# Four split weight blocks in a ring at all times, in place of two, with the new slots in the scratch of dynamic DMAs

## The chip, the cores and the metric

The kernel runs on one core of a Trainium2 chip. The metric is the device time of one execution in microseconds (us). TensorE (PE in the profile) multiplies matrices, VectorE (DVE) and ScalarE (ACT) do elementwise work, GpSimd (POOL) here does nothing but split weights, and SyncE (SP) issues the loads of weights. Each engine runs its own program; they meet at semaphores.

## What is computed

One inference step of a two-layer hybrid decoder trunk over 544 tokens (512 of a prompt, 8 x 4 of samples), in fp32. The reference, cut to its frame:

```python
def _swiglu(x, w_gate, w_up, w_down):
    return (jax.nn.silu(x @ w_gate) * (x @ w_up)) @ w_down

def _layer(x, state, p):
    f = _swiglu(_rmsnorm(x, p['ffn1_norm_pre']), p['ffn1_w_gate'], p['ffn1_w_up'], p['ffn1_w_down'])
    x = x + (0.5 * _rmsnorm(f, p['ffn1_norm_post'])).astype(x.dtype)
    m, new_state = _token_mixer(_rmsnorm(x, p['mix_norm_pre']), *state, p)
    x = x + _rmsnorm(m, p['mix_norm_post']).astype(x.dtype)
    f = _swiglu(_rmsnorm(x, p['ffn2_norm_pre']), p['ffn2_w_gate'], p['ffn2_w_up'], p['ffn2_w_down'])
    x = x + (0.5 * _rmsnorm(f, p['ffn2_norm_post'])).astype(x.dtype)
    return x, new_state
```

`_token_mixer` projects to the inputs of three recurrent branches (gated DeltaNet, GLA, Mamba-2), runs them, projects each branch's output, merges them by sigmoid gates and projects once more. The model width is 1024, the width of the feed-forward part 2816.

## The kernel before, in words

**Blocks.** Activations lie transposed in SBUF: 128 partitions of channels, 544 tokens along the free axis. A weight matrix is cut into blocks of up to 128 x 1024: eight tiles k of 128 x 128 that share one tile of output channels. To keep fp32 accuracy each operand is held as a rounded high part and a low part that is left over, and each tile takes six matmuls of 272 columns (`products`, lines 625 to 629): high by high, high by low, low by high, each for two halves of the tokens. A full block is 48 matmuls, a narrow one (tiles of the small columns, 128 x 256) is 12, a merge block (128 x 768) 36.

**The way of a block.** SP loads it into one of four slots of `raw` (512 KB for a full one). POOL splits it in two instructions: a conversion `wh<-raw` (TENSOR_SCALAR, line 586 or 572) and a subtraction `wl<-raw,wh` (TENSOR_TENSOR, line 588 or 574), which counts up `lo_done`. TensorE waits for `lo_done`, multiplies, and its last matmul counts up `blk_done`, which frees the split slot. `wh` and `wl` have two slots, so POOL may split block b+2 when block b is done.

**Two more slots for a while.** At the start of a feed-forward part TensorE takes three blocks side by side, tile k by tile k, because tile k of the input is ready before tile k+1. For that `whx` and `wlx` give slots to blocks 2 and 3. They lie in the memory of `al`, the low part of the feed-forward's inner activations, so they are free only behind the last block of the projection down of the part before. `first_blocks` on POOL splits these four blocks, in the order of FIRST_ORDER: 0, 1, 2, 3 in FFN 1 and 2, 3, 0, 1 in FFN 2, where `al` has been free since the merge.

**The order of the stages** in a layer, by its blocks: FFN 1 with 44 blocks up (gate and up in turn) and 24 down (a third of a tile row each: 8, 8, 6 tiles); the projection with 4 narrow blocks and 40 wide ones; the recurrent branches, in which no block is used and whose scratch covers `raw`, `wh` and `wl`; 48 merge blocks; 8 of the out projection (`wout`); FFN 2 like FFN 1.

**Borders between stages.** There TensorE waits for VectorE and ScalarE. VectorE scales and adds the result (`f` line 1951, `x` line 1956), and makes the low part `hl` of the next input (line 1931 in front of a feed-forward part, lines 1906 and 1912 in front of the projection, line 2525 in front of the merge). `xsq` (line 1942) sums the squares for the norm; TensorE takes its last tile through a matmul (line 693) in the middle of block 3 of the part up. In front of the merge the last updates of `states` (line 2205) must be four on before TensorE starts.

**Semaphores.** `blk_done` starts at SPLIT, and every wait that counts finished blocks adds SPLIT, so the same expressions hold for any depth of the ring.

Of the kernel before, what the change touches and what calls it, by code (L numbers as in the profile page):

```python
# [7 lines left out]
P = 128  # L8
# [5 lines left out]
KD = D_MODEL // P  # L14
# [46 lines left out]
RAW, SPLIT = 4, 2  # L61
# [82 lines left out]
FIRST_ORDER = (0, 1, 2, 3), (2, 3, 0, 1)  # L144


def split_count(which, j):

    return FIRST_ORDER[which].index(j) + 1

# [32 lines left out]
def trunk(nc, io):  # L183
    ctx = ExitStack()
    with ctx:
# [17 lines left out]

        x = put("x", [P, KD, T])
        RING = place[0]
        raw = put("raw", [P, RAW, KD, P])
        wh = put("wh", [P, SPLIT, KD, P], F32R)
        wl = put("wl", [P, SPLIT, KD, P], F32R)
# [230 lines left out]
        def _(sp_):  # L439
# [121 lines left out]
        def _(pool):  # L561
            def first_blocks(layer, which, first):

                for j in FIRST_ORDER[which]:
                    src = raw[:, j, :, :].rearrange("p k m -> p (k m)")
                    hi, lo = (a.rearrange("p k m -> p (k m)") for a in split_of(j, True))
                    pool.wait_ge(raw_full[j], layer * (BLOCKS // RAW * 16) + 16 * (first // RAW + 1))
# [4 lines left out]
                    pool.tensor_scalar(hi, src, 1.0, 1.0, MULT, MULT).then_inc(hi_done, 1)  # L572
                    pool.wait_ge(hi_done, layer * BLOCKS + first + split_count(which, j))
                    pool.tensor_tensor(lo, src, hi.bitcast(F32), SUB).then_inc(lo_done, 1)

            def blocks(layer, first, i, nks):

                for j, nk in enumerate(nks):
                    src = raw[:, j % RAW, 0:nk, :].rearrange("p k m -> p (k m)")
                    hi, lo = (a[:, 0:nk, :].rearrange("p k m -> p (k m)") for a in split_of(j, False))  # L580
# [29 lines left out]
        def _(pe):  # L610
            pe.wait_ge(first_in, 32)

            def products(j, slot, ks, moving, start, stop, ready=None, ahead=False, between=None):

                for n, k in enumerate(ks):
# [7 lines left out]
                    high, low = (w[:, k, :] for w in split_of(j, ahead))  # L623
# [8 lines left out]
            def product(layer, first, i, j, per, slot, nk, moving, start=True, stop=True, ready=None, ahead=False, between=None):  # L632
# [3 lines left out]
                products(j, slot, range(nk), moving, start, stop, ready, ahead, between).then_inc(blk_done, 1)  # L636
# [44 lines left out]
            def ffn(layer, which, first):  # L681

                def up(i, js=range(4)):
                    for j in js:

                        pe.wait_ge(prod_done if j % 2 else sil_done, value(pe, layer * (2 * KF) + i * 2 + (which * KF + j // 2 + 1)))
                        product(layer, first, i, j, 4, j, KD, h_tiles, ahead=i is FIRST,
                                between=all_squares if i is FIRST and j == 3 else None)
# [2040 lines left out]
```

## Time and profile before

| | before |
|---|---|
| median of 3 runs | 3318.38 us (3314.03 to 3329.16) |
| span of the profiled execution, first to last instruction | 3324.6 us |
| TensorE busy | 3162.4 us, 95% |
| VectorE busy | 1309.5 us, 39% |
| ScalarE busy | 776.6 us, 23% |
| GpSimd busy | 1577.5 us, 47% |
| HBM read | 243.70 MB |

The profiler took one execution. Its time is given as the span alone, which lies between the lowest and the highest of the timed runs. A busy share is a mean over stages; what a stall costs is read at its place. Matmuls overlap in the profile, so the mean duration of one (about 290 ns) is longer than the distance from one to the next (about 126 ns).

### The profile page before, as it was taken

The numbers are of one execution on the slowest core, as the hardware profiler recorded it, in microseconds if no ns is written. First come the engines' busy times: TensorE is split into PE (matmuls) and PEld (weight loads), VectorE is DVE, ScalarE is ACT, GpSimd is POOL, SyncE is SP. The second block draws the span as 40 slices with busy tenths as digits, with TensorE's granted clock in tenths as the row PEclk, the third lists the DMA queues.
The fourth block names the chain that finished last, engine by engine and source line by source line (L and its number), as shares of the span: only waits on it lengthen the run. The fifth ranks groups of instructions, "written<-read, shape, count | busy, mean of one in ns | idle before, by whom it ended". The sixth has DMA issues, their size and how long they took to land.

```text
span 3324.6 us, 67286 instructions
## 1 busy us (share of the span) xinstructions
PE 3162.4 (95%) x26882; PEld 3059.8 (92%) x26882; DVE 1309.5 (39%) x1984; ACT 776.6 (23%) x1523; POOL 1577.5 (47%) x948
## 2 busy tenths in 40 slices
PE   7999989999989998999999999999999899999997
PEld 7999979987769998999989999899877799899997
DVE  4331064637752225331053311735487422343311
ACT  2111033324441112111021111343344311221100
POOL 4665545620016664555546655556100256555553
PEclk9999999999979999999999999999999799999999
DMA  3222222200132222222222222222002322222221
GB/s 136 83 88 84 75 78 85 83 25 2 41 136 89 86 91 76 88 88 83 83 81 88 88 87 72 79 83 89 7 2 73 121 89 90 96 70 88 86 83 67
DMA packets 78589, 261.08 MB, mean 79 GB/s; under 512 B 8640, under 2 KB 10816, under 8 KB 77632
## 3 DMA queue, kind: packets, MB, share of 16 engines
q1 hardware_dynamic: 78112, 257.82, 24.0%
q8 instruction: 149, 2.44, 0.3%
q10 hardware_dynamic: 288, 0.49, 0.1%
q14 instruction: 40, 0.33, 0.0%
HBM read 243.70 MB, written 14.58 MB: 78 GB/s over the span
## 4 chain that ended last, share of the span: by engine, by line
PE 86%; DVE 8%; ACT 4%; issue 2%; DMA 0%; POOL 0%; DVEq 0%; SPq 0%; ACTq 0%; POOLq 0%
PE ps L625 25%; PE ps L627 25%; PE ps L629 25%; PE ps L766 1%; PE ps L727 1%; DVE cacc L2012 1%; PE ps L649 1%; DVE l_att L2265 1%; DVE x L1956 1%; PE ps L1032 1%; PE ps L976 1%; DVE f L1951 1%; ACT states L1495 0%; PE ps L759 0%; PE ps L1275 0%
## 5 line engine op out<-in xcount | busy, mean ns | idle before, releaser
L586 POOL TENSOR_SCALAR wh<-raw 128x1024 fp32r<-128x1024 f32 (+2 forms) x456 | 465.4, 1021 | 1636.4 <-PE ps L629 1107.4
L588 POOL TENSOR_TENSOR wl<-raw,wh 128x1024 fp32r<-128x1024 f32 (+2 forms) x456 | 1051.7, 2306 | 67.2 <-POOL wh L586 0.3
L625 PE MATMUL ps<-hh,wh 128*128 128x272 f32 x4768 | 998.2, 291 | 76.5 <-DVE hl L1931 25.8
L627 PE MATMUL ps<-hl,wh 128*128 128x272 f32 x4768 | 992.2, 290 | 0.0
L629 PE MATMUL ps<-hh,wl 128*128 128x272 f32 x4768 | 990.7, 289 | 0.0
L625 PEld LDWEIGHTS ps<-hh,wh 128*128 128x128 f32 x4768 | 755.8, 190 | 84.8 <-issue 55.8
L629 PEld LDWEIGHTS ps<-hh,wl 128*128 128x128 f32 x4768 | 755.3, 190 | 0.0
L627 PEld LDWEIGHTS ps<-hl,wh 128*128 128x128 f32 x4768 | 753.0, 189 | 0.0
L629 PE MATMUL ps<-ah,wl 128*128 128x272 f32 x1408 | 291.3, 288 | 0.0
L625 PE MATMUL ps<-ah,wh 128*128 128x272 f32 x1408 | 291.3, 288 | 0.0
L627 PE MATMUL ps<-al,wh 128*128 128x272 f32 x1408 | 291.1, 288 | 0.0
L1985 DVE TENSOR_TENSOR prod<-sil,ps 128x544 f32<-128x544 f32 x88 | 63.5, 721 | 421.2 <-PE ps L629 401.6
L1942 DVE TENSOR_TENSOR sq<-sq 128x544 f32<-128x544 f32 x36 | 31.3, 871 | 499.9 <-ACT sq L1436 499.9
L629 PEld LDWEIGHTS ps<-ah,wl 128*128 128x128 f32 x1408 | 221.6, 189 | 0.0
L625 PEld LDWEIGHTS ps<-ah,wh 128*128 128x128 f32 x1408 | 221.6, 188 | 0.0
L627 PEld LDWEIGHTS ps<-al,wh 128*128 128x128 f32 x1408 | 220.3, 188 | 0.0
L1991 DVE TENSOR_TENSOR al<-prod,ah 128x544 f32 x88 | 145.1, 1648 | 97.0 <-ACT ah L1451 97.0
L2012 DVE SCALAR_TENSOR_TENSOR cacc<-pad,cw,cacc 128x568 f32<-128x568 f32 x120 | 169.4, 1412 | 12.6
L1451 ACT ACTIVATE ah<-prod 128x544 f32 x88 | 58.1, 660 | 464.6 <-DVE prod L1987 464.6
L1436 ACT ACTIVATE sq<-ps 128x544 f32 x48 | 30.0, 625 | 553.3 <-PE ps L629 553.3
L2564 DVE TENSOR_TENSOR sg<-ps,rstd 128x544 f32<-128x544 f32 x48 | 34.8, 724 | 252.1 <-PE ps L629 252.1
L1982 DVE TENSOR_TENSOR sil<-ps,rstd 128x544 f32<-128x544 f32 x88 | 63.7, 724 | 146.8 <-PE ps L629 120.7
(430 smaller groups left out, 3552.0 us busy)
## 6 DMA issues: line engine op xcount, KB each, us to landing
raw<-in_up SPq DMA_DIRECT2D x176, 512.0 KB, 3.5
raw<-in_win SPq DMA_DIRECT2D x80, 512.0 KB, 3.5
raw<-in_merge SPq DMA_DIRECT2D x96, 384.0 KB, 3.0
raw<-in_down SPq DMA_DIRECT2D x64, 512.0 KB, 3.5
raw<-in_down SPq DMA_DIRECT2D x32, 384.0 KB, 3.1
raw<-in_wout SPq DMA_DIRECT2D x16, 512.0 KB, 3.4
states<-in_in_gdn SPq DMA_DIRECT2D x2, 2048.0 KB, 8.9
proj<-in_in_ssd SPq DMA_DIRECT2D x2, 2048.0 KB, 9.9
```

The lines of the kernel that those rows point to most:

```text
L586: pool.tensor_scalar(hi, src, 1.0, 1.0, MULT, MULT).then_inc(hi_done, 1)
L588: pool.tensor_tensor(lo, src, hi.bitcast(F32), SUB).then_inc(lo_done, 1)
L625: pe.matmul(out, high, mh_[:, c], start=a, stop=False)
L627: pe.matmul(out, high, ml_[:, c], start=False, stop=False)
L629: last = pe.matmul(out, low, mh_[:, c], start=False, stop=b)
L649: last = pe.matmul(ps[:, 6 + h, 0:HALF], ones, src[:, h * HALF:(h + 1) * HALF], start=start, stop=stop, skip_group_check=True)
L1451: act.activation(ah[:, bass.ds(i * 2 + j, 1), :].rearrange("p k t -> p (k t)"), prod[:, j, :], ACT.Copy).then_inc(ah_done, 1)
L1982: dve.tensor_tensor(halves(sil[:, j, :]), pair(2 * j), halves(rstd[:, :]), MULT).then_inc(gate_done, 1)
L1985: dve.tensor_tensor(halves(prod[:, j, :]), halves(sil[:, j, :]), pair(2 * j + 1), MULT).then_inc(prod_tmp, 1)
L1991: dve.tensor_tensor(al[:, m, :].rearrange("p k t -> p (k t)"), prod[:, j, :], ah[:, m, :].rearrange("p k t -> p (k t)").bitcast(F32), SUB) ...
L2012: last = dve.scalar_tensor_tensor(out=a, in0=pad[:, j, t:t + CW], scalar=cw[:, 4 * j + t:4 * j + t + 1], in1=a, op0=MULT, op1=ADD)
L2564: dve.tensor_tensor(halves(sg[:, u % 2, :]), pair(2 * u % 4), halves(rstd[:, :]), MULT).then_inc(gate_done, 1)
```

## The change

The ring has four split slots throughout. `whx` and `wlx` get memory of their own, 16 KB per partition, ahead of `x`. They hold slots 2 and 3; `wh` and `wl` keep 0 and 1. The room comes from the scratch that the program reserves for dynamic DMAs, set to 512 in the program's constructor. With four slots everywhere, block j of any stage goes to slot j % 4, POOL may split block b+4 when block b is done, and the special case at the start of a feed-forward part goes: `first_blocks` on POOL, FIRST_ORDER and `split_count`, and the four single loads on SP at the start of FFN 2.

```diff
-RAW, SPLIT = 4, 2
+RAW, SPLIT = 4, 4
...
-FIRST_ORDER = (0, 1, 2, 3), (2, 3, 0, 1)
...
+        whx, wlx = (put(s, [P, 2, KD, P], F32R) for s in ("whx", "wlx"))
         x = put("x", [P, KD, T])
...
-        whx, wlx = (at(s, R + 44 * TB + 8192 * i, [P, 2, KD, P], F32R) for i, s in enumerate(("whx", "wlx")))
-        assert 2 * 8192 <= 8 * TB
-
-        def split_of(j, ahead):
-            return (whx[:, j - 2], wlx[:, j - 2]) if ahead and j >= 2 else (wh[:, j % SPLIT], wl[:, j % SPLIT])
+        def split_of(j):
+            j %= SPLIT
+            return (whx[:, j - 2], wlx[:, j - 2]) if j >= 2 else (wh[:, j], wl[:, j])
...
-                if which:
-                    for j in range(4):
-                        sp_.wait_ge(lo_done, layer * BLOCKS + first + split_count(which, j) + RAW)
-                        ups(layer, which, first, 1, slice(j, j + 1))
-                with sp_.Fori(2 if which else 1, KF // 2) as i:
+                with sp_.Fori(1, KF // 2) as i:
                     ups(layer, which, first, i)
...
-                    if which and j >= SPLIT:
-                        pool.wait_ge(blk_done, layer * BLOCKS + B_OUT + SPLIT)
-                    else:
-                        pool.wait_ge(blk_done, layer * BLOCKS + first + min(j + 1, SPLIT))
...
             def ffn(layer, which, first):
-                first_blocks(layer, which, first)
+                blocks(layer, first, 0, (KD,) * 4)
...
-    nc = bacc.Bacc("TRN2", target_bir_lowering=False, num_devices=1)
+    nc = bacc.Bacc("TRN2", target_bir_lowering=False, num_devices=1, dynamic_dma_scratch_size=512)
```

No instruction is added or taken away on POOL or TensorE; the wait on `blk_done` in front of each conversion asks for two blocks less. At the start of FFN 2 the order of the splits changes too. On POOL, behind the loop over the out projection, before the change (`whx` and `wlx` are slots 2 and 3, in the memory of `al`):

```order
L572 TENSOR_SCALAR whx_70<-raw_50 128x1024 [waits blk_done,raw_full2]
L574 TENSOR_TENSOR wlx_71<-raw_50,whx_70 128x1024 [waits hi_done]
L572 TENSOR_SCALAR whx_70<-raw_50 128x1024 [waits blk_done,raw_full3]
L574 TENSOR_TENSOR wlx_71<-raw_50,whx_70 128x1024 [waits hi_done]
L572 TENSOR_SCALAR wh_51<-raw_50 128x1024 [waits blk_done,raw_full0]
L574 TENSOR_TENSOR wl_52<-raw_50,wh_51 128x1024 [waits hi_done]
L572 TENSOR_SCALAR wh_51<-raw_50 128x1024 [waits blk_done,raw_full1]
L574 TENSOR_TENSOR wl_52<-raw_50,wh_51 128x1024 [waits hi_done]
```

And at the same place after it:

```order
L561 TENSOR_SCALAR wh_53<-raw_52 128x1024 [waits blk_done,raw_full0]
L563 TENSOR_TENSOR wl_54<-raw_52,wh_53 128x1024 [waits hi_done]
L561 TENSOR_SCALAR wh_53<-raw_52 128x1024 [waits blk_done,raw_full1]
L563 TENSOR_TENSOR wl_54<-raw_52,wh_53 128x1024 [waits hi_done]
L561 TENSOR_SCALAR whx_49<-raw_52 128x1024 [waits blk_done,raw_full2]
L563 TENSOR_TENSOR wlx_50<-raw_52,whx_49 128x1024 [waits hi_done]
L561 TENSOR_SCALAR whx_49<-raw_52 128x1024 [waits blk_done,raw_full3]
L563 TENSOR_TENSOR wlx_50<-raw_52,whx_49 128x1024 [waits hi_done]
```

The four blocks are now split in their order, and each waits for one block of the out projection. At the end of the narrow blocks, in front of the wide ones, POOL's rows before the change are:

```order
L586 TENSOR_SCALAR wh_51<-raw_50 128x256 [waits blk_done,raw_full2]
L588 TENSOR_TENSOR wl_52<-raw_50,wh_51 128x256 [waits hi_done]
L586 TENSOR_SCALAR wh_51<-raw_50 128x256 [waits blk_done,raw_full3]
L588 TENSOR_TENSOR wl_52<-raw_50,wh_51 128x256 [waits hi_done]
L600 UNCONDITIONAL_BRANCH
```

And after it:

```order
L561 TENSOR_SCALAR whx_49<-raw_52 128x256 [waits blk_done,raw_full2]
L563 TENSOR_TENSOR wlx_50<-raw_52,whx_49 128x256 [waits hi_done]
L561 TENSOR_SCALAR whx_49<-raw_52 128x256 [waits blk_done,raw_full3]
L563 TENSOR_TENSOR wlx_50<-raw_52,whx_49 128x256 [waits hi_done]
L575 UNCONDITIONAL_BRANCH
```

The order is the same; narrow blocks 2 and 3 have slots of their own, and the first wide block shares its slot with narrow block 0 in place of narrow block 2. At the merge it is likewise: blocks 2 and 3 go to `whx` and `wlx`, which no branch uses as scratch, and wait for no merge block.

## Rows read from the trace of the kernel before

**Rows 1.** The page, parts 1 and 3: engines' busy time, and the main DMA queue

```profile
PE 3162.4 (95%) x26882; PEld 3059.8 (92%) x26882; DVE 1309.5 (39%) x1984; ACT 776.6 (23%) x1523; POOL 1577.5 (47%) x948
...
q1 hardware_dynamic: 78112, 257.82, 24.0%
```

**Rows 2.** Windows: us; busy us (count) of PE, PEld, DVE, ACT, POOL; PEclk; DMA

```profile
1300.00:1650.00 350.00, 350.00 (x2778) 350.00 (x2777) 80.19 (x83) 45.88 (x63) 207.74 (x120) 1.00 0.28 87
```

**Rows 3.** POOL's instructions grouped by shape: count, busy us, mean ns, idle

```profile
L588 POOL TENSOR_TENSOR wl<-raw,wh 128x1024 fp32r<-128x1024 f32 x320 | 808.4, 2526 | 47.5 <-POOL wh L586 0.2
L586 POOL TENSOR_SCALAR wh<-raw 128x1024 fp32r<-128x1024 f32 x320 | 349.0, 1091 | 806.4 <-PE ps L629 806.4
L588 POOL TENSOR_TENSOR wl<-raw,wh 128x768 fp32r<-128x768 f32 x128 | 236.1, 1845 | 19.0 <-POOL wh L586 0.2
L586 POOL TENSOR_SCALAR wh<-raw 128x768 fp32r<-128x768 f32 x128 | 111.3, 869 | 772.7 <-DMA raw<-in_merge 528.9 <-PE ps L629 243.8
```

**Rows 4.** TensorE's waits: us in total, times, longest

```profile
PE ps L625 <- DVE states L2205: 17.0, 2, 8.6
...
PE ps L625 <- DVE hl L1912: 12.5, 9, 3.9
...
PE ps L625 <- POOL wl L588: 2.8, 2, 1.6
```

**Rows 5.** Windows: narrow blocks of layer 1, and the start of the merge

```profile
2097.60:2101.30 3.70, 3.67 (x16) 3.65 (x17) 3.03 (x6) 0.66 (x1) 1.66 (x2) 0.54 0.60 203
...
976.60:981.20 4.60, 4.59 (x20) 4.59 (x21) 2.35 (x4) 0.00 (x0) 0.00 (x0) 0.50 0.41 171
```

**Rows 6.** Lines 1982 and 1987: duration in ns, min/median/max

```profile
L1982 DVE TENSOR_TENSOR sil<-ps,rstd x88: 709/724/727, 42.9 to 3164.3; 128x544 f32<-128x544 f32 x88
...
L1987 DVE TENSOR_TENSOR prod<-prod,rstd x88: 724/725/2417, 46.6 to 3171.2; 128x544 f32<-128x544 f32 x88
```

**Rows 7.** The chain that ended last: start us, us, ahead of FFN 2 and FFN 1

```profile
1248.29 1.12 DVE f L1951
...
1249.44 2.76 DVE x L1956
...
1662.38 1.44 DVE x L1956
1663.82 2.81 DVE f L1951
1666.63 1.47 DVE hl L1931
```

**Rows 8.** Timeline of DVE and PE: narrow blocks, first wide block, layer 0

```profile
445.13 0.72 DVE L1912 TENSOR_TENSOR hl<-hf,hh 128x544 fp32r<-128x544 f32 x1
...
450.48 2.23 DVE L1912 TENSOR_TENSOR hl<-hf,hh 128x544 fp32r<-128x544 f32 x2
...
452.76 0.52 PE L625 MATMUL ps<-hh,wh 128*128 128x272 f32 x2 [0.43 <-DVE hl L1912]
...
455.07 0.49 PE L625 MATMUL ps<-hh,wh 128*128 128x272 f32 x2 [1.28 <-POOL wl L588]
```

**Rows 9.** Timeline of DVE and PE: start of FFN 2, layer 0

```profile
1269.38 5.27 DVE L1942 TENSOR_TENSOR xsq<-xsq 128x544 f32<-128x544 f32 x7
...
1276.20 1.14 PE L693 MATMUL ps<-xsq,cst 128*128 128x240 f32 x6
```

**Rows 10.** Timeline of POOL and PE: in front of the merge, layer 0

```profile
969.02 1.88 POOL L588 TENSOR_TENSOR wl<-raw,wh 128x768 fp32r<-128x768 f32 x1
...
976.61 0.82 PE L625 MATMUL ps<-hh,wh 128*128 128x272 f32 x2 [8.44 <-DVE states L2205]
```

**Rows 11.** Tile raw, 955 to 975 us: issues of loads, time to landing

```profile
L450 SPq DMA_DIRECT2D raw<-in_merge x4: 344/431/527, 961.1 to 962.5; - x4
...
DMA to landing us min/median/max: 3.0/5.5/7.2
```

**Rows 12.** Tile nt_s, 965 to 975 us: durations in ns, min/median/max

```profile
L2456 DVE SCALAR_TENSOR_TENSOR nt_s<-nt_s,prm,nrs_s x4: 238/520/1787, 968.1 to 969.2; 128x32 f32<-128x32 f32 x4
```

More of the change, by code:

```diff
@@ L206, in trunk @@
         raw = put("raw", [P, RAW, KD, P])
-        wh = put("wh", [P, SPLIT, KD, P], F32R)
-        wl = put("wl", [P, SPLIT, KD, P], F32R)
+        wh = put("wh", [P, 2, KD, P], F32R)
+        wl = put("wl", [P, 2, KD, P], F32R)
         cst = put("cst", [P, NCONST])
@@ L561, in _ @@
         def _(pool):
[L562 to L567, printed above, removed]
-                    if which and j >= SPLIT:
-                        pool.wait_ge(blk_done, layer * BLOCKS + B_OUT + SPLIT)
-                    else:
-                        pool.wait_ge(blk_done, layer * BLOCKS + first + min(j + 1, SPLIT))
-                    pool.tensor_scalar(hi, src, 1.0, 1.0, MULT, MULT).then_inc(hi_done, 1)
-                    pool.wait_ge(hi_done, layer * BLOCKS + first + split_count(which, j))
-                    pool.tensor_tensor(lo, src, hi.bitcast(F32), SUB).then_inc(lo_done, 1)
             def blocks(layer, first, i, nks):
@@ L579, in blocks @@
                     src = raw[:, j % RAW, 0:nk, :].rearrange("p k m -> p (k m)")
-                    hi, lo = (a[:, 0:nk, :].rearrange("p k m -> p (k m)") for a in split_of(j, False))
+                    hi, lo = (a[:, 0:nk, :].rearrange("p k m -> p (k m)") for a in split_of(j))
                     turns = len(nks) // RAW
@@ L611, in _, with products @@
             pe.wait_ge(first_in, 32)
-            def products(j, slot, ks, moving, start, stop, ready=None, ahead=False, between=None):
+            def products(j, slot, ks, moving, start, stop, ready=None, between=None):
                 for n, k in enumerate(ks):
@@ L622, in products @@
                     halves_of = [(ps[:, 2 * slot + h, 0:HALF], slice(h * HALF, (h + 1) * HALF)) for h in range(2)]
-                    high, low = (w[:, k, :] for w in split_of(j, ahead))
+                    high, low = (w[:, k, :] for w in split_of(j))
                     for out, c in halves_of:
@@ L630, in products, with product @@
                 return last
-            def product(layer, first, i, j, per, slot, nk, moving, start=True, stop=True, ready=None, ahead=False, between=None):
+            def product(layer, first, i, j, per, slot, nk, moving, start=True, stop=True, ready=None, between=None):
                 pe.wait_ge(lo_done, value(pe, layer * BLOCKS + i * per + (first + j + 1 + RAW)))
-                products(j, slot, range(nk), moving, start, stop, ready, ahead, between).then_inc(blk_done, 1)
+                products(j, slot, range(nk), moving, start, stop, ready, between).then_inc(blk_done, 1)
             def h_split(layer, number):
@@ L686, in up @@
                         pe.wait_ge(prod_done if j % 2 else sil_done, value(pe, layer * (2 * KF) + i * 2 + (which * KF + j // 2 + 1)))
-                        product(layer, first, i, j, 4, j, KD, h_tiles, ahead=i is FIRST,
-                                between=all_squares if i is FIRST and j == 3 else None)
+                        product(layer, first, i, j, 4, j, KD, h_tiles, between=all_squares if i is FIRST and j == 3 else None)
                 def all_squares():
@@ L703, in first_blocks @@
                             if k == 0:
-                                pe.wait_ge(lo_done, layer * BLOCKS + first + split_count(which, j) + RAW)
-                            last = products(j, j, (k,), lambda n: h_tiles(k), k == 0, k == KD - 1, ahead=True)
+                                pe.wait_ge(lo_done, layer * BLOCKS + first + j + 1 + RAW)
+                            last = products(j, j, (k,), lambda n: h_tiles(k), k == 0, k == KD - 1)
                             if k == KD - 1:
```

2 lines of the change are left out of this document (removed).

## The prediction

> **What bounds the kernel now.** I read the page first: TensorE is busy for 3162.4 of 3324.6 us, GpSimd (POOL), which makes every split, for 1577.5 us [rows 1]. So the sum of the matmuls sets the time, and only what makes TensorE stand still can change it. The windows of the long stages say the same: TensorE was busy 350.00 of 350.00 us in one [rows 2]. There a ring of two slots already suffices: a split of a full block takes 1.09 + 2.53 us [rows 3], and a block of 48 matmuls takes 48 x 350 / 2778 = 6.05 us [rows 2]. The split for the block after next starts when a block ends and is over well before it is needed. With four slots the split of block b+4 starts when block b ends: the same instant, the same work. The long stages stay as they are.
>
> Then I read the list of TensorE's waits. POOL's split is the releaser of only 2.8 us, twice in the program; the waits that matter are for VectorE (DVE), 17.0 us for `states` and 12.5 for `hl` of line 1912 among them [rows 4]. So the change can touch little directly. What it does move is when POOL works at the borders between stages, and there DVE is the engine on the path. How the two engines disturb each other is the heart of the case, and three readings show it:
> - `sil` (line 1982) reads one operand from PSUM and never took over 727 ns in 88 times; `prod` (line 1987) reads two from SBUF, has a median of 725 ns and took up to 2417 [rows 6]. An operation of DVE with two SBUF operands is held by POOL, one that reads PSUM is not.
> - The chain of what ended last shows at 1249.44 an `x` of 2.76 us and at 1663.82 an `f` of 2.81 us [rows 7], where such an operation alone takes 0.72 us (the row of 445.13 in [rows 8]). POOL was in a subtraction of 2.4 us or more each time. DVE stands until POOL's instruction is over.
> - In turn, POOL's next instruction waits for the one of DVE that is running. Where both have work, they alternate.
> So a microsecond of split that lies in a stretch where DVE prepares the next stage costs TensorE about a microsecond.
>
> **The change part by part.** The four borders, each twice or once in the program.
>
> (E) *From FFN 2 to FFN 1 of layer 1, once.* Today blocks 2 and 3 wait for the last down block, because their slots lie in the memory of `al`, so three splits run in the tail. On the path DVE needs `x` 1.44, `f` 2.81 and `hl` 1.47 us [rows 7], against about 0.72 to 0.78 each when free: 5.7 - 2.2 = 3.5 us are holds. After the change only one split is left behind the last down block, at the same time as block 1's today, and it is over when DVE begins. Gain 3.5, less a hold of 0.1 for its end. The matmul of the sums also waited 0.2 us for `xsq`, which goes. E = -3.6 us.
>
> (B) *From the out projection to FFN 2, twice.* Today POOL makes four splits in a queue behind the last `wout` block; the last reaches into DVE's tail: `f` 1.12, `x` 2.76, so 1.12 + 2.76 - 1.44 = 2.4 us of hold [rows 7]. After, blocks 0 to 2 are split as `wout` blocks 4 to 6 end, and only block 3 in the tail; it takes its 3.6 us right behind the last `wout` block and, by my estimate, reaches 0.2 to 0.5 us into DVE's first operation. TensorE starts 2.4 - 0.3 = 2.1 us earlier. But then the ring gives back: the split of block 4 waits for block 0 in place of block 2, so it comes 1.5 us earlier within the stage, while the seven additions of `xsq` still run (1269.38 to 1274.65, and TensorE asks for their sum at 1276.20: 1.55 us of slack) [rows 9]. Conversion and subtraction, 3.6 us, hold them for some 3.0 us (POOL itself waits for one addition first). 3.0 - 1.55 = 1.4 us of new wait. B = -2.1 + 1.4 = -0.7 each, -1.4 in all. Ends: 0 and -2.4 each.
>
> (A) *From FFN 1 to the projection, twice.* This is where the ring should help: the first wide block waits for POOL, 1.28 us in layer 0 [rows 8] and 1.6 in the other [rows 4], since its split may start only behind narrow block 2. After the change it may start behind narrow block 0, at 445.13, and that of wide block 1 behind narrow block 1, which ends while the first is split. So POOL has two full splits on hand, 2 x (1.09 + 2.53) = 7.2 us, at the very moment at which DVE still has eight operations to do for `hl` 3 to 7. Today these eight end at 452.71, in 7.6 us, with short splits of 256 columns beside them [rows 8]. Alone they are 8 x 0.66 = 5.3 us (each is shown with 0.72, of which its neighbour overlaps 0.06). With 7.2 us of POOL between them 12.5 us, the end is at 457.6 in place of 452.7. The last two thirds of a step on TensorE stand behind it (from 452.76 on, 1.0 us), so the first wide block starts at 458.6, not at 455.07: +3.5 us, and the POOL wait is gone. Ends: +2.7 (one conversion fits in a gap of DVE) and +4.5 (the conversion of wide block 2 comes in front of the last `hl`, 1.09 more). A = +3.5 each, +7.0 in all. If no hold arose at all, it would be the -1.4 that the ring was to give.
>
> (C) *From the mixer to the merge, twice.* POOL has waited for `in_merge`. Today it makes two splits and stops, since both slots are full; its last subtraction ends at 969.02 + 1.88 = 970.90, and from there DVE does its last row norms, `hl` and `states` freely; TensorE starts at 976.61 behind the fourth `states` [rows 10]. After, splits 2 and 3 follow at once: their data are landed (the four loads land 3.0 to 7.2 us after issue, the last issue at 962.5) [rows 11]. That is 2 x (0.87 + 1.85) = 5.4 us of POOL [rows 3] against nine operations of DVE with SBUF operands, which stand in program order ahead of the `states` that TensorE wants. Small ones slip in while POOL changes instruction: of the four of line 2456 one took 1787 ns, but another 238 [rows 12]. So I take 4.8 of the 5.4. C = +4.8 each, +9.6 in all. Ends: +2.7 (only one split falls ahead of the last SBUF operation) and +5.4. The page "SBUF — State Buffer" of the Trainium skill, section "Who interferes with whom", says that whoever issues first gets the shared pair for the whole instruction and the other fully blocks. By that alone the hold at C would be all of POOL's four instructions, and the sum 1 us more; the trace agrees that the loser stands still, and adds that short operations find gaps.
>
> (D) *Start of the program.* The four splits are the same, in the same order. The split of block 4 comes after block 0, while DVE adds up `xsq`; but here TensorE takes one block after the other and has two full ones to do before it asks for the sums, 12 us. 0.
>
> The address of `x`, `raw` and the rest moves; no row shows a cost that depends on it. The scratch of dynamic DMAs is cut from the default to 512. 257.82 of 261 MB go through q1, whose kind is hardware_dynamic, issued by SyncE [rows 1]. The Trainium skill ("SBUF — State Buffer", "SBUF size: 192, 224, or 256?") calls that scratch the ring of descriptors of software-made DMAs; by that page nothing here would notice. 0, and a raw block is landed long before it is split.
>
> **Sum.** -3.6 - 1.4 + 7.0 + 9.6 = +11.6 us, on the profiled 3324.6 us. That execution lies inside the three timed ones (3314.03 to 3329.16), so I add the sum to the median: 3318.4 + 11.6 = 3330 us. With all ends: low -3.7 - 4.8 + 5.4 + 5.4 = +2.3, high -3.4 + 0 + 9.0 + 10.8 = +16.4.
>
> **The rivals.**
> - *Slower, the clock (3338).* At A in layer 1 TensorE fell to a granted clock of 0.54, the lower level, 1.2 GHz, for 3.7 us, behind short waits for `hl` [rows 5]. If DVE feeds it with gaps of 3 to 4 us, it runs its last narrow step (6 matmuls, 0.6 us more) and the first 4.6 us of the wide block at the lower level (as it did for the 4.6 us of 976.60, clock 0.50 [rows 5], 20 matmuls that at full clock are 2.5 us: 2.1 to 2.3 more). A becomes 6.4 each. With C at its end of 5.4, B at -0.4 and E at -3.3: 12.8 + 10.8 - 0.8 - 3.3 = +19.5, 3338 us. It decides from A of 5.0 each on, with the others so. For it: layer 1 shows the fall; against: in layer 0 the pair at 452.76 took 0.52 us [rows 8], so there the level was the higher one.
> - *Faster, the holds don't come (3307).* DVE gets ahead at A and C, as it does in short gaps today, or the data of merge blocks 2 and 3 land late. A then is -1.4 each, C 0, B -2.4 each, E -3.6: -3.6 - 4.8 - 2.8 = -11.2, 3307 us. Against it: at 1663 and 1249 DVE was held by full instructions every time.
> - *No change (3318).* Gains at B and E equal what A and C cost, A and C at their low ends: +2, 3320 us. This is also what comes if wide splits at A start late because POOL computes the waits in registers.
> - *Cut scratch slows the loads (over 3340).* Then all loads would land later; but a block is asked for when its slot is free and split four blocks on, 24 us at 6.05 each, so a load would have to take over 20 us to be seen, and those of [rows 11] took 7.2 at most.
>
> **How the numbers follow.** My forecast 0.62, slower by the clock 0.16, no change 0.11, faster 0.10, scratch 0.01. A change under 0.5%, 16.6 us, can hardly be told from none by this measurement. The forecast lies within it, with a tail of 0.03 above; no change and most of the faster case (11 us) too. Slower by over 0.5%: 0.15 + 0.03 = 0.18; faster by over 0.5%: 0.03; same 0.79. The likeliest case alone reaches from 3320 to 3335 (+2 to +16). The range takes in half of the faster case and most of the clock's: 3310 to 3340.
>
> **What would show it.** In the changed profile: at E `x`, `f`, `hl` near 0.75 us and one split only in the tail; at B `x` under 1 us, but a wait of some 1.5 us ahead of the sums' matmul; at A no wait for POOL, `hl` operations of 2.5 to 3 us, the last `hl` 4 to 5 us later than now; at C four splits in a row and TensorE's wait for `states` 13 us in place of 8.44. Waits by line: `hl` of line 1912 up from 12.5 us to some 20, `states` from 17 to 27. I am wrong if A and C show DVE's operations at their free length beside POOL's subtraction, or if TensorE's pace in the long stages changes.

## The result, and the profile after

The kernel after takes 3331.14 us (median of 4 runs, 3326.76 to 3339.49) against 3319.57 us for the kernel before, run on the same chip (4 runs, 3314.03 to 3329.16): ratio 1.0035, 95% interval 1.0019 to 1.0052, so 11.6 us slower. In a second measurement it took 3332.73 us against 3321.93, ratio 1.0034 (1.0021 to 1.0047).

The two profiled executions differ far less, 3325.0 and 3324.6 us of span. The borders between stages cost 11.2 us more in the new one, and the stages between them ran 10.8 us faster, 5.0 of it in one stage. That second difference is the spread from one execution to the next, with either ring (figures below the table). In this case a single pair of traces gives the right borders and the wrong total.

The page of the kernel after, part 1, answers to [rows 1]:

```profile
PE 3158.4 (95%) x26882; PEld 3056.5 (92%) x26882; DVE 1331.3 (40%) x1984; ACT 776.3 (23%) x1523; POOL 1576.4 (47%) x948
```

The counts are the same on every engine. POOL's busy time is the same but for 1.1 us. DVE's grew by 21.8 us with the same 1984 instructions: they are held. TensorE's waits after, in us in total, times and longest (the second fence is from the kernel before):

```profile
PE ps L600 <- DVE states L2179: 25.3, 2, 12.7
PE ps L600 <- DVE hl L1886: 18.6, 6, 3.9
PE ps L600 <- DVE hl L1905: 17.9, 7, 4.9
```

```profile
PE ps L625 <- DVE hl L1931: 25.8, 6, 8.3
```

(Lines are 25 or 26 less than before: 1912 is now 1886, 1931 is 1905, 2205 is 2179.) Against [rows 4] the wait for `states` grew from 17.0 to 25.3 and that for `hl` in front of the projection from 12.5 to 18.6. The wait for `hl` in front of the feed-forward parts fell from 25.8 to 17.9: that is where the ring gives something back. The 2.8 us for POOL are gone; all that is left for POOL is the program's start, 11.7 us (12.0 before).

**From FFN 1 to the projection, layer 0.** The timeline of POOL, DVE and TensorE after, answering to [rows 8]:

```profile
441.52 1.53 POOL L561 TENSOR_SCALAR wh<-raw 128x1024 fp32r<-128x1024 f32 x1 [22.90 <-PE ps L604]
443.19 2.63 POOL L563 TENSOR_TENSOR wl<-raw,wh 128x1024 fp32r<-128x1024 f32 x1
445.80 1.52 POOL L561 TENSOR_SCALAR wh<-raw 128x1024 fp32r<-128x1024 f32 x1
447.46 2.63 POOL L563 TENSOR_TENSOR wl<-raw,wh 128x1024 fp32r<-128x1024 f32 x1
...
442.06 1.56 DVE L1880 SCALAR_TENSOR_TENSOR hf<-x,prm,rstd 128x544 f32<-128x544 f32 x1
443.54 2.86 DVE L1886 TENSOR_TENSOR hl<-hf,hh 128x544 fp32r<-128x544 f32 x1
446.33 1.56 DVE L1880 SCALAR_TENSOR_TENSOR hf<-x,prm,rstd 128x544 f32<-128x544 f32 x1
447.81 2.86 DVE L1886 TENSOR_TENSOR hl<-hf,hh 128x544 fp32r<-128x544 f32 x1
...
446.55 0.49 PE L600 MATMUL ps<-hh,whx 128*128 128x272 f32 x2 [2.63 <-DVE hl L1886]
450.73 0.82 PE L600 MATMUL ps<-hh,whx 128*128 128x272 f32 x2 [2.86 <-DVE hl L1886]
455.86 0.49 PE L600 MATMUL ps<-hh,wh 128*128 128x272 f32 x2 [1.20 <-ACT proj L1763]
```

The two engines alternate, instruction by instruction: each `hf` spans the rest of a conversion, each `hl` a whole subtraction. The last row holds what I had not foreseen: once POOL is no longer late, the first wide block still waits 1.20 us, for ScalarE to copy the narrow blocks' result (`proj`, line 1763) out of PSUM. Before, that copy was made too:

```profile
453.82 0.62 ACT L1789 ACTIVATE proj<-ps 128x544 f32<-128x544 f32 x1 [2.57 <-PE ps L629]
```

It ended at 454.44. After, the copy ended at 455.31 and TensorE started 0.55 us behind it; the same 0.55 before would be 454.99, and TensorE started at 455.07.

**From the mixer to the merge, layer 0**, POOL, DVE and TensorE, answering to [rows 10] and [rows 12]:

```profile
967.54 1.88 POOL L563 TENSOR_TENSOR wl<-raw,wh 128x768 fp32r<-128x768 f32 x1
969.39 0.82 POOL L561 TENSOR_SCALAR whx<-raw 128x768 fp32r<-128x768 f32 x1
970.36 1.91 POOL L563 TENSOR_TENSOR wlx<-raw,whx 128x768 fp32r<-128x768 f32 x1
972.24 0.87 POOL L561 TENSOR_SCALAR whx<-raw 128x768 fp32r<-128x768 f32 x1
973.26 2.34 POOL L563 TENSOR_TENSOR wlx<-raw,whx 128x768 fp32r<-128x768 f32 x1
...
970.65 2.60 DVE L2483 TENSOR_TENSOR nt_s<-nt_s,proj 128x128 f32<-128x128 f32 x2
973.17 0.77 DVE L2499 SCALAR_TENSOR_TENSOR hl<-x,prm,hh 128x544 fp32r<-128x544 f32 x1
974.02 2.13 DVE L2440 TENSOR_TENSOR ol<-nt_s,oh 128x128 fp32r<-128x128 f32 x3
...
979.29 0.82 PE L600 MATMUL ps<-hh,wh 128*128 128x272 f32 x2 [12.59 <-DVE states L2179]
```

The same two groups of small operations before:

```profile
971.51 0.49 DVE L2509 TENSOR_TENSOR nt_s<-nt_s,proj 128x128 f32<-128x128 f32 x2
...
972.77 0.69 DVE L2466 TENSOR_TENSOR ol<-nt_s,oh 128x128 fp32r<-128x128 f32 x3
```

POOL runs on for two splits, `nt_s` x2 takes 2.60 us (0.49 before), `ol` x3 2.13 (0.69 before), and TensorE waits 12.59 in place of 8.44.

**From FFN 2 to FFN 1 of layer 1**, DVE and TensorE, answering to [rows 7]:

```profile
1662.80 0.73 DVE L1930 SCALAR_TENSOR_TENSOR x<-f,x 128x544 f32<-128x544 f32 x1
1663.44 0.78 DVE L1925 SCALAR_TENSOR_TENSOR f<-f,prm,rstd_post 128x544 f32<-128x544 f32 x1
1664.34 0.79 DVE L1905 SCALAR_TENSOR_TENSOR hl<-x,wpre,hh 128x544 fp32r<-128x544 f32 x1
```

All three are at their free length, as forecast.

For each border I take the time from a fixed event ahead of it to a fixed one behind it (differences of start times in the traces, us). Start: first matmul to block 4 of FFN 1 (counted from 0: the first block of the second turn, which waits for `sil`). A: matmuls of the sums to the first wide block. Projection: from there to the branches' first matmul with a long wait. C: TensorE's wait for `states`. B and E: DVE's first `f` to block 4 of the next part up. "again" is a second trace of the kernel after; the rest are experiments. What is far from its neighbours is set bold.

| | start | A, layers 0, 1 | projection | C | B | E |
|---|---|---|---|---|---|---|
| before | 34.0 | 26.9, 27.4 | 257.5, 255.7 | 8.4, 8.6 | 34.2, 34.2 | 37.3 |
| after | 35.0 | 32.0, 32.1 | 255.7, 255.6 | 12.6, 12.7 | 32.5, 33.3 | 32.0 |
| again | 33.0 | 31.9, 31.8 | 255.9, 257.5 | 12.6, 12.7 | 33.2, 32.5 | 33.2 |
| scratchBefore | 34.4 | 27.3, 27.0 | 257.5, 255.7 | 8.4, 8.6 | 34.0, 35.0 | 37.2 |
| lateA | 34.3 | 25.9, 25.6 | **265.5, 263.8** | 12.8, 12.7 | 32.5, 33.3 | 32.7 |
| lateC | 33.8 | 32.1, 32.1 | 257.4, 259.2 | 8.5, 8.5 | 32.7, 33.3 | 32.8 |
| lateAC | 34.1 | 25.8, 25.6 | **266.0, 264.5** | 8.5, 8.5 | 33.4, 33.3 | 31.8 |
| shortA | 34.4 | 25.8, 25.4 | 256.8, 257.5 | 12.6, 12.7 | 32.3, 33.2 | 33.8 |
| projMerge | 34.2 | 25.8, 26.0 | 259.0, 257.4 | 8.5, 8.5 | 33.3, 32.7 | 32.0 |
| onlyB | 34.1 | 25.6, 25.6 | 256.8, 256.8 | 8.5, 8.5 | 32.3, 32.7 | **37.2** |
| projMergeStart | **29.7** | 26.1, 25.6 | 257.4, 257.5 | 8.5, 8.5 | 32.4, 34.1 | 32.8 |
| bestAgain | **29.8** | 25.5, 26.1 | 256.8, 257.2 | 8.5, 8.5 | 33.4, 33.3 | 32.0 |
| bestTurn1 | **29.7** | 25.5, 25.6 | 257.6, 257.5 | 8.5, 8.5 | 32.4, 31.7 | 32.7 |
| startOnly | **30.1** | 31.9, 32.3 | 255.7, 259.1 | 12.6, 12.7 | 32.6, 32.6 | 32.8 |

Before against after: start +1.0, A +5.1 and +4.7, C +4.2 and +4.1, B -1.7 and -0.9, E -5.3; together +11.2, where the timed medians differ by 11.6.

The long stages don't know of the ring. Block 4 of FFN 1 to the sums of layer 0 took 382.2 us before and 377.2 after, but also 377.2 with the old ring (scratchBefore) and 382.2 in one trace with four slots (startOnly). All that lies outside the borders (the projection counts as outside) took 3113.7 us before and 3102.9 after, but also 3101.7 in scratchBefore and 3118.6 in startOnly.

### The profile page after: what moved, and what is told of

The parts are those of the page before. It is cut to its first block, busy times and chain, and to the rows that moved or that the text cites. A ratio compares the mean times of both kernels' runs of the same rounds, so it can differ in the third digit from the quotient of the medians.

```text
span 3325.0 us, 67314 instructions
## 1 busy us (share of the span) xinstructions
PE 3158.4 (95%) x26882; PEld 3056.5 (92%) x26882; DVE 1331.3 (40%) x1984; ACT 776.3 (23%) x1523; POOL 1576.4 (47%) x948
## 4 chain that ended last, share of the span: by engine, by line
PE 84%; DVE 9%; ACT 4%; issue 2%; DMA 0%; DVEq 0%; ACTq 0%; SPq 0%
PE ps L600 24%; PE ps L602 24%; PE ps L604 24%; DVE cacc L1986 2%; PE ps L740 1%; PE ps L624 1%; PE ps L701 1%; DVE l_att L2239 1%; PE ps L1006 1%; PE ps L950 1%; DVE hl L1886 0%; ACT states L1469 0%; DVE cacc L1983 0%; PE ps L733 0%; PE ps L1249 0%
## 5 line engine op out<-in xcount | busy, mean ns | idle before, releaser
L600 PE MATMUL ps<-hh,wh 128*128 128x272 f32 x2448 | 514.6, 292 | 71.8 <-DVE states L2179 25.3
L563 POOL TENSOR_TENSOR wl<-raw,wh 128x1024 fp32r<-128x1024 f32 (+2 forms) x236 | 547.3, 2319 | 34.2 <-POOL wh L561 0.2
L563 POOL TENSOR_TENSOR wlx<-raw,whx 128x1024 fp32r<-128x1024 f32 (+2 forms) x236 | 544.3, 2306 | 34.2 <-POOL whx L561 0.2
L600 PE MATMUL ps<-hh,whx 128*128 128x272 f32 x2448 | 508.5, 289 | 10.9 <-DVE hl L1886 10.9
L602 PE MATMUL ps<-hl,wh 128*128 128x272 f32 x2448 | 512.3, 291 | 0.0
L604 PE MATMUL ps<-hh,wl 128*128 128x272 f32 x2448 | 509.9, 290 | 0.0
L602 PE MATMUL ps<-hl,whx 128*128 128x272 f32 x2448 | 507.6, 289 | 0.0
L604 PE MATMUL ps<-hh,wlx 128*128 128x272 f32 x2448 | 505.9, 288 | 0.0
L600 PEld LDWEIGHTS ps<-hh,whx 128*128 128x128 f32 x2448 | 385.7, 189 | 13.2 <-DVE hl L1886 6.3
L604 PEld LDWEIGHTS ps<-hh,wlx 128*128 128x128 f32 x2448 | 386.3, 189 | 0.0
L1986 DVE SCALAR_TENSOR_TENSOR cacc<-pad,cw,cacc 128x568 f32<-128x568 f32 x120 | 176.6, 1472 | 12.6
```

The costliest lines, as they stand in the source:

```text
L600: pe.matmul(out, high, mh_[:, c], start=a, stop=False)
L602: pe.matmul(out, high, ml_[:, c], start=False, stop=False)
L604: last = pe.matmul(out, low, mh_[:, c], start=False, stop=b)
L1986: last = dve.scalar_tensor_tensor(out=a, in0=pad[:, j, t:t + CW], scalar=cw[:, 4 * j + t:4 * j + t + 1], in1=a, op0=MULT, op1=ADD)
```

## The experiments

**Undoing the ring at single borders.** A block in the list `late` waits for two more finished blocks, that is, as in a ring of two (`further` adds SPLIT); slots and addresses stay those of the kernel after. lateA has the first of the two calls below (the first turn taken out of its loop), lateC the second, lateAC both.

```diff
-            def blocks(layer, first, i, nks):
+            def blocks(layer, first, i, nks, late=()):
...
-  pool.wait_ge(blk_done, further(pool, layer * BLOCKS + i * len(nks) + (first + j + 1)))
+  pool.wait_ge(blk_done, further(pool, layer * BLOCKS + i * len(nks) + (first + j + 1 + 2 * (j in late))))
...
-                with pool.Fori(0, 10) as i:
+                blocks(layer, B_PROJ + 4, 0, (KD,) * 4, late=(0, 1, 2, 3))
+                with pool.Fori(1, 10) as i:
...
-                with pool.Fori(0, KD // 2) as i:
+                blocks(layer, B_MERGE, 0, (6, 6) * 6, late=(2, 3))
+                with pool.Fori(1, KD // 2) as i:
```

**The kernel after once more** (again).

> The change itself, again, for a tighter ratio. Theory (POOL's earlier splits hold VectorE at the borders): slower than before by 8 to 14 us of 3320. Rival (the difference is only the pace of the long stages from run to run): within 4 us of before.

Measured 3332.73 us, ratio 1.0034, 10.8 us slower than before, as expected.

**Merge blocks 2 and 3 late** (lateC).

> The change, but merge blocks 2 and 3 wait for merge blocks 0 and 1. Theory: TensorE's wait for states falls from 12.6 us to 8.4 twice, 8.3 us under the change, +3 against before. Rival (the longer wait comes from the DMAs of raw and states, which meet now): the wait stays near 12.

Measured 3323.15 us, ratio 1.0003 (0.9991 to 1.0016), 9.6 less than again. TensorE's wait at the merge is back:

```profile
978.47 0.82 PE L601 MATMUL ps<-hh,wh 128*128 128x272 f32 x2 [8.45 <-DVE states L2180]
```

C is settled: splits 2 and 3, made too early, cost 8.3 us by the traces, 9.6 by the timed medians. (The late blocks' loads are asked for later as well, so the run alone doesn't part splits from loads. The rows above do: DVE's operations grew by as much as TensorE's wait.)

**The first four wide blocks late** (lateA).

> The change, but the first four wide blocks of the projection wait for two blocks more, as in a ring of two. Theory: the hl of line 1912 are free again, the first wide block starts at the last hl plus some 2 to 4 us, so A's +9.8 goes to about -3 and the whole comes 10 to 13 us under the change, -1 to +2 us against before. Rival (the clock, or TensorE's own waits, makes A): hl still 2.8 us long and no gain.

Measured 3333.62 us, ratio 1.0042 (1.0029 to 1.0056): no gain, against the expectation. Yet the border did become short (25.9 and 25.6 us, `hl` at 0.72). The time went away again in the projection, 265.5 and 263.8 us. The trace of DVE and POOL in its first group:

```profile
465.05 7.14 DVE L1987 SCALAR_TENSOR_TENSOR cacc<-pad,cw,cacc 128x568 f32<-128x568 f32 x3
472.11 1.31 DVE L1984 TENSOR_SCALAR cacc<-pad,cw 128x568 f32<-128x568 f32 x1
...
467.17 1.56 POOL L561 TENSOR_SCALAR wh<-raw 128x1024 fp32r<-128x1024 f32 x1
468.87 2.71 POOL L563 TENSOR_TENSOR wl<-raw,wh 128x1024 fp32r<-128x1024 f32 x1
471.55 1.55 POOL L561 TENSOR_SCALAR wh<-raw 128x1024 fp32r<-128x1024 f32 x1
```

With only four late blocks POOL owes two when the loop begins, and makes them up back to back: a split every 4.3 us (from 467.17 to 488.48, five distances) in place of every 6.0. The convolutions' chain on DVE (`cacc`, three operations) takes 7.14 us; with one split beside it, in the kernel after, it took 4.59 (at 470.20). The first group of four tiles takes 29.5 us (from 459.62) where the kernel after takes 21.9, and TensorE meets the delay 80 us later, at the sums over the keys, by way of ScalarE:

```profile
546.11 3.97 PE L1250 MATMUL ps<-proj,cst 128*128 128x272 f32 x8 [4.77 <-ACT proj L1787]
```

Behind that wait TensorE runs at the lower level of its clock, 1.2 GHz. A window of lateA:

```profile
546.10:551.80 5.70, 5.70 (x17) 4.77 (x18) 0.40 (x1) 3.29 (x6) 0.00 (x0) 0.50 0.27 92
```

In shortA, 5.70 us from the same matmul on hold 41 matmuls at a granted clock of 1.00. At 0.126 us each, the 24 matmuls less are some 3 us, an estimate; with the wait they make up most of the 8 to 10 us.

**Both** (lateAC).

> Both together: the ring of four where it takes splits out of a tail, a ring of two where it would put splits into one. Theory: the two add up, 18 to 21 us under the change and 6 to 10 us under before, so faster than both. Rival: the gains at the starts of FFN 1 and FFN 2 are given back later, and it comes out at before's time.

Measured 3327.85 us, ratio 1.0021 (1.0008 to 1.0034), 4.9 under again where 18 to 21 was expected, 5.9 above before where 6 to 10 under it was: against the expectation. It is 4.7 more than lateC, with the same long projection. Two readings fit: the backlog holds DVE, or a TensorE that comes 6 us early only meets the convolutions' chain. The next runs tell them apart.

**Shorter splits, no backlog** (shortA). All waits of the kernel after; the projection's first four wide blocks split only their first tile. The split of the other seven tiles is left out, and TensorE multiplies what their slots held, so the results are not the reference's:

```diff
+                blocks(layer, B_PROJ + 4, 0, (KD,) * 4, only=1)
+                with pool.Fori(1, 10) as i:
```

> The kernel after, with the splits of the projection's first four wide blocks cut to 128 of 1024 columns each (the rest of them is left out, so these four blocks' products are not the reference's). Everything else waits and is ordered as after. Theory (it is the time that POOL's splits hold DVE): hl and hf of these 11 us unheld (0.75 us each), first wide block about 5 us earlier (border about 26 to 27 in place of 32), and since POOL has no backlog the projection stays at about 523 us: near 3323, 10 less than the kernel after. Rival one (the order of the waits, not the holds): border 32, 3333. Rival two (a TensorE that comes early to the projection only waits later for the convolutions' chain on DVE, whatever POOL does): border 27 but 528 us and a new wait at the key sums, 3330.

Measured 3316.92 us, ratio 0.9987 (0.9974 to 1.0000), 15.8 less than again, where 10 was expected. DVE and POOL at the border:

```profile
445.76 0.98 DVE L1888 TENSOR_TENSOR hl<-hf,hh 128x544 fp32r<-128x544 f32 x1
...
444.49 0.78 POOL L562 TENSOR_SCALAR wh<-raw 128x128 fp32r<-128x128 f32 x1 [22.71 <-PE ps L606]
445.35 0.81 POOL L564 TENSOR_TENSOR wl<-raw,wh 128x128 fp32r<-128x128 f32 x1
```

Same order, same waits; only the length of POOL's instructions changed, `hl` fell from 2.86 to 0.98, and A is 25.8 and 25.4 us. So A is the duration of holds. TensorE comes just as early as in lateA, and the projection stays at 256.8 and 257.5: the long projection of lateA was the backlog. TensorE's wait in front of the first wide block is 1.20 us here too. The profile puts it down to POOL, whose split of that block was over at 446.16; the length fits ScalarE's copy. (A explains 12.5 of the 15.8 us; the rest is within what two medians from different groups of runs can differ by.)

**No backlog, full splits** (projMerge). All forty wide blocks late, and merge blocks 2 and 3:

```diff
                 with pool.Fori(0, 10) as i:
-                    blocks(layer, B_PROJ + 4, i, (KD,) * 4)
+                    blocks(layer, B_PROJ + 4, i, (KD,) * 4, late=(0, 1, 2, 3))
```

> All forty wide blocks of the projection wait as in a ring of two, and so do blocks 2 and 3 of the merge's first turn; the ends of the two FFNs keep the ring of four. Theory (POOL's extra splits cost where they run beside DVE's serial work, and a backlog that is let go later costs there again): without a backlog the operations cacc of the first group stay at 4.6 us for three in place of the 7.14 that the run with only four late blocks had; first wide block to merge about 521 us a layer, the border FFN1 to projection near 27 as before, states wait 8.4; left over are the border FFN2 to FFN1 at -5.3, two borders out projection to FFN2 at -1.3 each and the start at +1.0, so about 3315 us beside 3322 of before. Rival one (the projection grew because TensorE came to it early, not by the backlog): 530 us a layer again, 3325 to 3330. Rival two (the addresses of the slots or the smaller scratch cost something everywhere): 3322 or more.

Measured 3313.56 us, ratio 0.9974 (0.9962 to 0.9985), faster than both kernels. The projection is back at 259.0 and 257.4. What is left of the change is what it gives at B and E.

**The ring of two at FFN 1's start as well** (onlyB).

The numbers in `waits` are the counts of finished blocks that blocks 0 to 3 wait for.

```diff
-                blocks(layer, first, 0, (KD,) * 4)
-                with pool.Fori(1, KF // 2) as i:
+                blocks(layer, first, 0, (KD,) * 4, waits=None if which else (3, 4, 4, 4))
+                with pool.Fori(1, 2) as i:
+                    blocks(layer, first, i, (KD,) * 4, late=() if which else (0, 1, 2, 3))
+                with pool.Fori(2, KF // 2) as i:
...
```

> As projMerge, and FFN1's first two turns wait as in a ring of two as well, in both layers: the border FFN2 to FFN1 and the start are as before the change, only the ends of the out projections keep the ring of four. Theory: projMerge + 5.3 - 1.0 = 4 us more than projMerge, about 3319, with the PE's wait for the first hl of layer 1 back from 4.9 to about 8 us. Rival (the border FFN2 to FFN1 gives nothing in the timed runs, the gain of 5.3 is chance of one execution): same as projMerge.

Measured 3316.32 us, ratio 0.9979 (0.9966 to 0.9992): 2.8 more than projMerge, where 4 was expected, with intervals that overlap. By its time alone nothing is told apart. Its trace does: E is 37.2 us again, as in both traces with the old ring, where each of the other traces with four slots in the table has 31.8 to 33.8, and TensorE's wait for `hl` is partly back:

```profile
PE ps L603 <- DVE hl L1908: 21.7, 7, 8.2
```

**The program's start** (projMergeStart; bestAgain is the same kernel once more; startOnly has this edit alone on the kernel after).

```diff
-                blocks(layer, first, 0, (KD,) * 4)
+                blocks(layer, first, 0, (KD,) * 4, late=(2, 3) if layer + which == 0 else ())
```

> As projMerge, with blocks 2 and 3 of the very first turn late, so that POOL doesn't split them while DVE makes the squares xsq of layer 0 (10.95 us for seven in place of 7.49). Theory: start 1 us shorter, about 3314. Rival: the two splits come later in a backlog and hold the first products of FFN1 instead; no difference to projMerge or 1 us more.

> The kernel of projMergeStart once more, word for word. Its trace showed the first FFN's border 4.5 us shorter than projMerge's, its time 7 us less, in six executions only. Theory (only what the traces show is real): about 3309, ratio near 0.996. Rival (the 3306.5 stands): ratio 0.9947 again.

> The kernel after, with nothing changed but blocks 2 and 3 of the very first turn, which wait as in a ring of two. Theory (each border's cost stands by itself): the start alone, 35.0 to 30 us, so 4 to 5 us less than after: about 3328. Rival (the borders work on each other by TensorE's clock or by the phase of the splits): anything but 3326 to 3330.

Measured: projMergeStart 3306.54 us, ratio 0.9947 (0.9927 to 0.9968); bestAgain 3308.35, ratio 0.9959 (0.9944 to 0.9975); startOnly 3325.98, ratio 1.0011 (1.0001 to 1.0022), 5.2 and 6.8 us under the two measurements of the kernel after; about 3328 was expected, and it lies at the edge of what its rival allowed. From projMerge to projMergeStart I had expected 1 us; the traces show 4.5 and the timed medians 7.0 (5.2 with bestAgain). The size was wrong because the reason was: I had counted on a freer `xsq`, and what became free is `hl`. The kernel before and the kernel after both split four blocks while DVE prepares the first input; the first fence is before, the second projMergeStart, `hl` and `xsq` on DVE:

```profile
13.69 9.72 DVE L1931 SCALAR_TENSOR_TENSOR hl<-x,wpre,hh 128x544 fp32r<-128x544 f32 x5 [0.41 <-ACT hh L1426]
23.33 7.49 DVE L1942 TENSOR_TENSOR xsq<-xsq 128x544 f32<-128x544 f32 x7
```

```profile
13.54 5.99 DVE L1906 SCALAR_TENSOR_TENSOR hl<-x,wpre,hh 128x544 fp32r<-128x544 f32 x5 [0.40 <-ACT hh L1401]
19.45 8.23 DVE L1917 TENSOR_TENSOR xsq<-xsq 128x544 f32<-128x544 f32 x7
```

`hl` is 3.7 us shorter and `xsq` no shorter. TensorE, fed sooner, also kept its clock: from 22.40 to 25.80 it was granted 0.50 before (15 matmuls) and 1.00 in projMergeStart (30 matmuls).

**Blocks 0 and 1 of FFN 2's second turn late as well** (bestTurn1).

```diff
-                with pool.Fori(1, KF // 2) as i:
+                with pool.Fori(1, 2) as i:
+                    blocks(layer, first, i, (KD,) * 4, late=(0, 1) if which else ())
+                with pool.Fori(2, KF // 2) as i:
...
```

> As bestAgain, with blocks 0 and 1 of the second turn of FFN2 late in both layers, so that POOL doesn't split them while DVE makes xsq (8.83 us for seven in the trace of projMergeStart, 4.9 to 6.0 unheld, and TensorE waits 2.43 for it in one layer). Theory: up to 2.4 us a layer less, 1 to 3 us less than bestAgain in all. Rival: the two splits then fall on the first operations of the second turn (sil, prod, al) and nothing is left: the same as bestAgain.

Measured 3305.27 us, ratio 0.9952 (0.9938 to 0.9966). In front of FFN 2 `xsq` is free in both layers (5.28 us for seven, where bestAgain has 8.20 and 8.15), and B is 32.4 and 31.7 (bestAgain 33.4 and 33.3). Its 3.1 us on bestAgain agree with the theory, but lie within the intervals. It is the fastest kernel of the study together with projMergeStart.

**The old ring on the new memory** (scratchBefore).

```diff
+        spare = put("spare", [P, 2, 2, KD, P])
         x = put("x", [P, KD, T])
...
-    nc = bacc.Bacc("TRN2", target_bir_lowering=False, num_devices=1)
+    nc = bacc.Bacc("TRN2", target_bir_lowering=False, num_devices=1, dynamic_dma_scratch_size=512)
```

> The kernel before, with the scratch of the dynamic transfers cut to 512 bytes and a spare array of 16 KB a partition put ahead of x, so that all addresses behind it are those of the kernel after; the ring and its order stay. Theory: same as before, within 0.1%. Rival (the cut scratch slows the loads or the addresses cost something): 3324 or more, raw loads of over 6.9 us median.

Measured 3319.37 us, ratio 0.9997 (0.9985 to 1.0008), and its loads of `raw` land as those of before do (2.2/3.4/11.1 there):

```profile
DMA to landing us min/median/max: 2.2/3.4/10.9
```

Scratch and addresses cost nothing that this measurement can tell. In the Trainium skill's terms ("SBUF — State Buffer", section "SBUF size: 192, 224, or 256?") the ring of descriptors that was cut serves software-made transfers, and here q1, of a hardware kind, carries nearly all bytes [rows 1]; the run agrees.

## Why the prediction was right

The forecast was 3330 us, +11.6; measured were 3331.14 and +11.6. The mechanism is the one forecast: POOL's earlier splits hold DVE at A and C, and fewer splits hold it at B and E. That the sum agrees to a tenth is luck. The terms were less exact, and their errors cancel:

| term | forecast | in the traces | |
|---|---|---|---|
| E, once | -3.6 | -5.3 | right in kind |
| B, both | -1.4 | -2.6 | right in kind |
| A, both | +7.0 | +9.8 | outside its ends, 2.7 to 4.5 each |
| C, both | +9.6 | +8.3 | right |
| D | 0 | +1.0 | chance, see below |
| sum | +11.6 | +11.2 | |

**C.** Four splits in a row, and waits of 12.6 and 12.7 against a forecast of 13; `states` in total 25.3 against 27. lateC undid it and nothing else: -9.6 us. The step "I take 4.8 of the 5.4" should have read 4.1 to 4.2: `nt_s` (line 2435, 1.23 for 0.60), `nt_s` (line 2483) and `ol` grew by 0.6, 2.1 and 1.4 us, and the `hl` between them ran at its free 0.77.

**A.** The holds came as written: from the sums' matmul to the last `hl`'s end DVE needed 4.5 us more than before (4.9 forecast). What failed is the step "the last two thirds of a step on TensorE stand behind it (..., 1.0 us), so the first wide block starts at 458.6". Between the last `hl`'s end, at 452.81, and the first wide block lie 3.05 us. The end of the narrow blocks ran partly at the lower level of the clock, 1.2 GHz (granted 0.50 from 450.70 to 453.00), as these windows of the kernel after show (busy time and count by engine, granted clock, DMA):

```profile
450.70:454.80 4.10, 3.93 (x18) 3.72 (x18) 3.02 (x6) 0.77 (x2) 2.03 (x2) 0.62 0.56 182
454.80:458.30 3.50, 2.44 (x19) 2.47 (x20) 0.00 (x0) 0.52 (x1) 3.35 (x3) 1.00 0.26 74
```

and then came the 1.20 us for ScalarE's copy. TensorE's own work behind `hl` took 1.85 us where I had 1.0, and the copy came on top. So 2.05 us more behind `hl` and 0.45 less ahead of it: 5.1 in place of 3.5. The copy was there before too, hidden behind POOL's 1.28 us: without POOL's wait TensorE would have started only some 0.1 us sooner (454.99 for 455.07, above). The 1.28 and 1.6 us that the ring was to give were therefore nearly worthless: it took one wait away and the next, as long, stood behind it. The part of the clock rival that speaks of the narrow blocks came true (0.62 there), its 4.6 us of the wide block did not in this trace (granted clock 1.00 from 454.80 on). In lateC's, with the same A, it did:

```profile
455.00:458.50 3.50, 3.46 (x15) 3.49 (x16) 0.00 (x0) 0.00 (x0) 3.23 (x2) 0.50 0.45 150
```

This falls behind A as I measure it, into the projection: 257.4 us there, 255.7 in the kernel after. So part of the clock rival was real, and smaller than it said.

**E.** All three operations became free. Expected was a gain of 3.6; the border gained 5.3, 3.4 of it ahead of the first matmul, where TensorE waits 4.87 in place of 8.27. Most of the other 1.9 us are TensorE's clock behind that wait, a term that the forecast of E left out. The first 9 us of TensorE before, after, and in the second trace of the kernel after:

```profile
1668.35:1677.35 9.00, 9.00 (x49) 8.84 (x50) 8.63 (x10) 3.89 (x6) 2.01 (x1) 0.66 0.01 2
```

```profile
1665.38:1674.38 9.00, 9.00 (x60) 9.00 (x61) 8.51 (x13) 5.19 (x8) 0.00 (x0) 0.81 0.01 2
```

```profile
1660.69:1669.69 9.00, 9.00 (x50) 9.00 (x51) 8.51 (x13) 5.19 (x8) 0.00 (x0) 0.67 0.01 2
```

The 11 matmuls more, at 0.126 us each, are 1.4 us (an estimate), and another 0.2 is the wait for `xsq` that went. The third window shows that this part differs by execution: with the same wait of 4.87 the clock came back later, and E is 33.2 there. In the ten other traces with the ring of four at this place the border is 31.8 to 33.8, a gain of 3.4 to 5.5. onlyB put the border back to 37.2 us. The timed difference, 2.8 us, doesn't settle it alone.

**B.** The hold on `x` is gone (0.72), TensorE's first wait is 4.87 in place of 7.22. The new hold on `xsq` comes in some executions and not in others: 5.99 and 8.09 us for seven additions in the two layers of the kernel after, 5.27 before; TensorE waited for them once, 0.9 us (1.4 once in again), where I had 1.4 in each layer. The clock takes back some more: 52 and 55 matmuls in the first 9 us, where before has 57 and 58. So -0.7 each was one draw of a term between 0 and -2.4; bestTurn1 takes the hold away.

**D.** "TensorE ... has two full ones to do before it asks for the sums" held. `xsq` was held, 10.95 us in place of 7.49, and was over at 34.48, 5.8 us before TensorE came to its sums:

```profile
23.53 10.95 DVE L1916 TENSOR_TENSOR xsq<-xsq 128x544 f32<-128x544 f32 x7
...
40.25 1.14 PE L667 MATMUL ps<-xsq,cst 128*128 128x240 f32 x6
```

So the +1.0 is chance: a second trace of the same kernel has 33.0, and projMerge, with `xsq` at 13.05 us, has 34.2. What I did not ask is whether the start could be better than before. Its splits hold DVE in both kernels, and that was worth 4.5 us.

**The rivals.** Faster would have needed A and C unheld; shortA and lateC show that they were held. No change is out by the interval. The clock's 3338 needed A at 6.4; it was 4.9 on average. Loads slowed by the cut scratch: scratchBefore, no.

## What to carry to other kernels

A deeper ring gives nothing where the shallow one is never waited for; it moves work earlier, and the question is what runs beside it there. An engine that works ahead and shares a way into memory with the engine on the path should be paced: let it work ahead where the other is idle (here, ahead of the feed-forward parts), and hold it back where the other prepares the next stage. When you hold it back, hold it for the whole stage: work that is owed comes back to back and costs the same again elsewhere. And before you count a removed wait as a gain, ask which wait stands behind it, and at which clock TensorE runs after it.

## What the runs showed of the hardware

- *Which operations of DVE are held.* I had written that those with two SBUF operands are. Operations with one are held too. A copy of 16 columns on DVE took 2.30 us beside a subtraction of POOL (lateA; at 452.65 in the kernel before too, where its shortest is 0.17), and `cacc` of line 2009 (TENSOR_SCALAR, one tensor operand, before) took 2.65 us at 493.82, where its shortest is 0.50 and its median 0.63:

```profile
446.76 2.30 DVE L1976 COPY cw<-prm 128x16 f32 x1
```

```profile
493.82 2.65 DVE L2009 TENSOR_SCALAR cacc<-pad,cw 128x568 f32<-128x568 f32 x1
```

The Trainium skill ("SBUF — State Buffer", "Who interferes with whom") has it so: copies and TENSOR_SCALAR can enter a mode with two ports and then contend. The rows agree.
- *The turns.* With work on both sides POOL and DVE took turns, one instruction each, and each was longer for the other: DVE's `hl` 2.86 us in place of 0.72, POOL's conversion 1.53 in place of 1.04. What a hold costs is set by the number of pairs and the length of POOL's instruction, so splits of 128 columns (0.8 us) did little harm.
- *TensorE's clock behind a wait.* In front of the feed-forward parts TensorE ran for some time at 1.2 GHz behind its wait for `hl`. In the 9 us behind it came 49 matmuls after a wait of 8.27 us (E, before), 57 after 7.22 (B, before), and 60, 50 and 52 after 4.87 (E after, E again, B after). A border's cost goes on behind its last wait, by an amount that a single trace doesn't fix.
- *The pace of the long stages* differed between executions, with either ring: from 377.0 to 383.5 us for FFN 1 from block 4 to its sums in the fourteen traces, more than most of the terms of this case.
